# Attention values products with the values stationary in two column tiles, on a hybrid decoder trunk

## The reference

```python
# FoX: 4 heads, own keys and values per head, causal, a forget bias
logits = einsum('bqhd,bkhd->bhqk', qb, k) * scale + Fq[..., None] - Ft[:, :, None, :]
p = softmax(where(causal, logits, -inf)); out = einsum('bhqk,bkhd->bqhd', p, v)
...
# DSA: 4 query heads, one key and one value head, only the 256 best keys of an indexer
p = softmax(logits); out = einsum('bhqk,bqkd->bqhd', p, vg)
...
# sliding window: 4 query heads on 2 key and value heads, the last 128 keys, a sink in the softmax
p = softmax(concatenate([logits, sink]))[..., :-1]; out = einsum('bnhgqs,bnshd->bnqhgd', p, vb)
...
ys = stack([y_a, y_d, y_f, y_s]); proj = einsum('blnc,ncd->blnd', ys, w_branch)
out = sum(sigmoid(g) * proj) @ w_o
```

## Time and profile before

| | |
|---|---|
| median of 3 runs | 1719.34 us (1719.2 to 1725.06) |
| span of the profiled execution | 1720.7 us |
| PE busy | 1674.9 us, 97% of the span |
| DVE, ACT, POOL busy | 62%, 36%, 48% |
| first FoX stretch, from the first to the last turning | 261.2 to 296.0 us |
| second FoX stretch | 340.5 to 374.8 us |
| window units | 376.8 to 406.3 us |
| DSA units | 759.6 to 830.0 us |

### The profile page before, as it was taken

The page is one execution under the profiler, slowest core; times in us unless marked ns, Lnnn a source line. Parts: engine busy times, 40 slices in busy tenths (PEclk is TensorE's granted clock), DMA queues, the critical chain, the costliest instruction groups (busy, mean ns, idle before and its releaser), DMA issues.

```text
span 1720.7 us, 22891 instructions
## 1 busy us (share of the span) xinstructions
PE 1674.9 (97%) x8072; PEld 1394.3 (81%) x8072; DVE 1058.8 (62%) x1756; ACT 612.9 (36%) x1104; POOL 822.9 (48%) x537
## 2 busy tenths in 40 slices
PE   5999999999999999999999999999999999999997
PEld 4877878788888888879888888888888888888886
DVE  7745985565999999567586445743453354345337
ACT  5543326274223222246323454322223222322323
POOL 2421130101436665540387334776567556655855
PEclk9999998999999999999999999999999999999999
DMA  8131141001111111320674412121112012111205
GB/s 345 37 84 39 62 108 28 31 25 45 61 46 46 46 46 50 137 77 1 246 261 159 171 54 94 37 74 49 49 49 73 24 49 73 49 49 49 73 25 208
DMA packets 37600, 138.89 MB, mean 81 GB/s; under 512 B 4640, under 2 KB 4768, under 8 KB 37536
## 3 DMA queue, kind: packets, MB, share of 16 engines
q1 hardware_dynamic: 35296, 130.70, 21.7%
q0 software_dynamic: 2240, 7.34, 1.9%
HBM read 118.10 MB, written 13.63 MB: 77 GB/s over the span
## 4 chain that ended last, share of the span: by engine, by line
PE 87%; DVE 6%; ACT 2%; DMA 1%; SPq 1%; issue 1%; DVEq 1%; POOL 0%; POOLq 0%; ACTq 0%
PE ps L662 25%; PE ps L663 25%; PE ps L664 25%; PE ps L888 4%; PE ps L867 2%; PE ps L789 1%; PE ps L790 1%; DMA region_a<-in_x 1%; PE ps L693 1%; DVE region_c L1966 1%; SPq L549 1%; DVE h_t L1958 0%; DVEq L2016 0%; DVE region_a L2318 0%; DVE top L2012 0%
## 5 line engine op out<-in xcount | busy, mean ns | idle before, releaser
L662 PE MATMUL ps<-h_t,w_t 128*128 128x512 f32 x1112 | 436.8, 393 | 1.8 <-DVE h_t L1958 1.6
L664 PE MATMUL ps<-h_t,w_t 128*128 128x512 f32 x1112 | 433.5, 390 | 0.0
L663 PE MATMUL ps<-h_t,w_t 128*128 128x512 f32 x1112 | 433.5, 390 | 0.0
L662 PEld LDWEIGHTS ps<-h_t,w_t 128*128 128x128 f32 x1112 | 209.2, 188 | 47.3 <-issue 2.5
L1616 POOL TENSOR_TENSOR w_t<-raw,w_t 128x1280 fp32r<-128x1280 f32 (+1 forms) x50 | 141.5, 2830 | 216.1 <-ACT w_t L1197 215.8
L664 PEld LDWEIGHTS ps<-h_t,w_t 128*128 128x128 f32 x1112 | 209.2, 188 | 43.8
L663 PEld LDWEIGHTS ps<-h_t,w_t 128*128 128x128 f32 x1112 | 209.1, 188 | 42.9 <-issue 0.7
L2333 DVE TENSOR_TENSOR y_f<-ps,y_f 128x512 f32<-128x512 f32 x120 | 80.8, 686 | 217.5 <-PE ps L664 217.5
L1775 POOL TENSOR_TENSOR w_t<-raw,w_t 128x512 fp32r<-128x512 f32 x80 | 110.8, 1390 | 135.9 <-ACT w_t L1504 135.6
L2012 DVE MAX8 top<-region_b 128x8 f32<-128x512 f32 (+5 forms) x192 | 159.2, 883 | 20.4 <-issue 19.7
L2015 DVE MATCH_REPLACE8 region_b<-top,region_b 128x512 f32<-128x512 f32 (+5 forms) x192 | 166.4, 877 | 0.0
(11 more groups left out here) (287 smaller groups left out, 3344.8 us busy)
## 6 DMA issues: line engine op xcount, KB each, us to landing
raw<-in_w_ffn SPq DMA_DIRECT2D x46, 512.0 KB, 3.9
raw<-in_w_gates SPq DMA_DIRECT2D x32, 640.0 KB, 4.0
region_b<-in_w_ada SPq DMA_DIRECT2D x33, 512.0 KB, 4.5
region_d<-in_w_ffn SPq DMA_DIRECT2D x20, 512.0 KB, 4.1
raw<-in_w_z SPq DMA_DIRECT2D x18, 512.0 KB, 3.4
region_a<-in_x SPq DMA_DIRECT2D x8, 512.0 KB, 14.8
h_f<-in_w_ada SPq DMA_DIRECT2D x8, 512.0 KB, 8.7
raw<-in_w_o SPq DMA_DIRECT2D x8, 512.0 KB, 3.6
```

What stands on the lines that cost most here:

```text
L662: pe.matmul(o, a_hi, m_hi, start=first, stop=False, skip_group_check=more)
L663: pe.matmul(o, a_hi, m_lo, start=False, stop=False, skip_group_check=more)
L664: return pe.matmul(o, a_lo, m_hi, start=False, stop=last, skip_group_check=more)
```

## The change

The output of a group is now made with channels on partitions from the start: the values are stationary (64 columns), 128 columns of turned probabilities move, and the two heads of a group write the two halves of the partitions of one bank, as two column tiles of the array (`rows_of` 0 and 1). Both units of a pair are multiplied in one go at the pair's end, so a DSA group has two heads now and there are 16 of them. What is turned on PE is no longer the output but the reciprocal of the denominators, spread over 64 columns each (`group_over_den`); DVE then copies the turned reciprocals out of PSUM and multiplies the output with them (`group_norm`, into `y_raw`). For the window that result is final, and its `group_lo` is gone. On PE a round is now: logits of u + 2, `turn_out` and values of u - 1, turning of u. The scratch of the descriptors of POOL's DMAs is halved to 8192 bytes to make room for `y_raw`.

```diff
-            return O_DSA + TT - 1 - b, h == 0, h == HEADS - 1
+            return O_DSA + 2 * (TT - 1 - b) + h // 2, h % 2 == 0, h % 2 == 1
...
+            def turn_out(u):
+                g, _, last = group_of(u)
+                if not last:
+                    return
+                if g >= 2:
+                    pe.wait_ge(s_y_raw, g - 1)
+                pe.wait_ge(s_y_tok, g + 1)
+                for c in range(BT if units[u][0] == "swa" else 1):
+                    mm = pe.transpose(group_bank(u)[:, BW + c * P:BW + (c + 1) * P],
+                                      y_tok[g % 2][:, c * P:(c + 1) * P], ident)
+                mm.then_inc(s_turned, 1)
+
             def values(u):
-                g, first, last = group_of(u)
+                if not group_of(u)[2]:
+                    return
                 pe.wait_ge(s_pt, u + 1)
-                if first and g >= 2:
-                    pe.wait_ge(s_of, g - 1)
...
-                        mm = pe.matmul(bank[:, col * HD:(col + 1) * HD], pt[u % 2][:, c * P:(c + 1) * P],
-                                       vn[:, block_, v0:v0 + HD], start=n == 0, stop=n == len(terms) - 1)
+                    for c in range(b + 1):
+                        for j, rows_ in enumerate(rows_of):
+                            v0 = VF + (h - 1 + j) * HD if kind == "fox" else VD
+                            mm = pe.matmul(bank[rows_, 0:P], vn[:, c, v0:v0 + HD],
+                                           pt[(u - 1 + j) % 2][:, c * P:(c + 1) * P], start=c == 0, stop=c == b)
...
                     if u + 2 < end:
                         logits(u + 2)
-                    turn(u)
+                    if u > u0:
+                        turn_out(u - 1)
+                        values(u - 1)
                     if u >= end - 2:
                         fill(parts_at[2 * (u - end + 2)])
-                    if u - 2 >= u0:
-                        turn_out(u - 2)
-                    if u > u0:
-                        values(u - 1)
+                    turn(u)
...
                     if u >= u0 + 2:
-                        act.wait_ge(s_pv, u - 1)
+                        act.wait_ge(s_pv, group_of(u - 2)[0] + 1)
...
-            def group_norm(u):
+            def group_over_den(u):
...
-                dve.wait_ge(s_pv, u + 1)
+                dve.wait_ge(s_exp, u + 1)
...
-                                  group_bank(u)[:, 0:nh * HD].rearrange("p (h d) -> p h d", h=nh),
-                                  r.unsqueeze(2).broadcast_to((P, nh, HD)), ALU.mult).then_inc(s_y_tok, 1)
+                dve.tensor_copy(y_tok[g % 2][:, 0:nh * HD].rearrange("p (h d) -> p h d", h=nh),
+                                r.unsqueeze(2).broadcast_to((P, nh, HD))).then_inc(s_y_tok, 1)
+
+            def group_norm(u):
...
+                dve.wait_ge(s_pv, g + 1)
+                dst, turned, over_den = group_values(u, y_s)
+                if kind != "swa":
+                    dst = y_raw[:, g % 2, :]
+                order.then_wait(dve.tensor_copy(dst, turned))
+                dve.tensor_tensor(dst, over_den, dst, ALU.mult).then_inc(s_y_raw, 1)
...
                         biased(u + 1)
+                    if u > u0:
+                        group_over_den(u - 1)
                     if u >= u0 + 2:
                         group_norm(u - 2)
...
-    nc = bacc.Bacc("TRN2", target_bir_lowering=False, num_devices=1)
+    nc = bacc.Bacc("TRN2", target_bir_lowering=False, num_devices=1, dynamic_dma_scratch_size=8192)
```

More of the change, by code:

```diff
@@ L83 @@
 O_FOX, O_SWA, O_DSA = 0, 2 * TT, 3 * TT
+O_END = O_DSA + 2 * TT
 MIX0 = 1
@@ L391, in build @@
         s_turned = sem("s_turned")
+        s_y_raw = sem("s_y_raw")
         s_o_hi = sem("s_o_hi")
@@ L594, in _ @@
             for dt, (s, n) in enumerate(((s_logit, after), (s_logit, after), (s_lg, after), (s_t, after - 1), (s_t, after),
-                                         (s_pv, after - 1), (s_pv, after)), 1):
+                                         (s_pv, O_END), (s_pv, O_END)), 1):
                 sp.wait_ge(s, n)
@@ L901, in turn_out, with values @@
                 mm.then_inc(s_turned, 1)
+            def values(u):
+                kind, b, h = units[u]
+                if not group_of(u)[2]:
+                    return
+                pe.wait_ge(s_pt, u + 1)
+                bank = group_bank(u)
+                if kind == "swa":
+                    cs = (0, 1) if b else (1,)
+                    for ch in range(BT):
+                        for n, c in enumerate(cs):
+                            for j, rows_ in enumerate(rows_of):
+                                k0, v0 = (2 * (2 * ch + j) + c) * P, VS + ch * HD
+                                mm = pe.matmul(bank[rows_, ch * P:(ch + 1) * P], vn[:, b - 1 + c, v0:v0 + HD],
+                                               pt[u % 2][:, k0:k0 + P], start=n == 0, stop=n == len(cs) - 1)
+                else:
+                    for c in range(b + 1):
+                        for j, rows_ in enumerate(rows_of):
+                            v0 = VF + (h - 1 + j) * HD if kind == "fox" else VD
+                            mm = pe.matmul(bank[rows_, 0:P], vn[:, c, v0:v0 + HD],
+                                           pt[(u - 1 + j) % 2][:, c * P:(c + 1) * P], start=c == 0, stop=c == b)
+                mm.then_inc(s_pv, 1)
             def attention(u0, n, gate=None, halves=0):
@@ L926, in attention @@
                 fill(parts_at[4])
-                turn_out(end - 2)
+                turn_out(end - 1)
                 values(end - 1)
                 fill(parts_at[5])
-                turn_out(end - 1)
                 fill(4 * KT)
@@ L1315, in group_hi @@
                     return
-                act.wait_ge(s_turned, g + 1)
-                dst, src = group_turned(u, y_hi(1 if units[u][0] == "fox" else 0))
-                act.activation(dst, src, ACT.Copy).then_inc(s_o_hi, 1)
+                act.wait_ge(s_y_raw, g + 1)
+                dst, _, _ = group_values(u, y_hi(1 if units[u][0] == "fox" else 0))
+                act.activation(dst, y_raw[:, g % 2, :], ACT.Copy).then_inc(s_o_hi, 1)
             def exponentials(u):
@@ L2096, in group_norm @@
                     return
-                nh = 2 if kind == "fox" else HEADS
-                dve.wait_ge(s_pv, u + 1)
+                nh = HEADS if kind == "swa" else 2
+                dve.wait_ge(s_exp, u + 1)
                 d, r = den[:, g % 4, 0:nh], rec[:, g % 2, 0:nh]
@@ L2113, in group_lo @@
                     return
[L2114 to L2122 removed]
+                dve.wait_ge(s_pv, g + 1)
[4 more added lines that the diff above has]
+                dve.tensor_tensor(dst, over_den, dst, ALU.mult).then_inc(s_y_raw, 1)
+            def group_lo(u):
+                kind, b, h = units[u]
+                g, _, last = group_of(u)
+                if not last or kind == "swa":
+                    return
+                buf = 1 if kind == "fox" else 0
+                dve.wait_ge(s_o_hi, split_group(u) + 1)
+                dst, _, _ = group_values(u, y_lo(buf))
+                hi, _, _ = group_values(u, y_hi(buf))
+                dve.tensor_tensor(dst, y_raw[:, g % 2, :], hi.bitcast(F32), ALU.subtract).then_inc(s_of, 1)
             def biased(u):
@@ L2168, in attention @@
                         group_lo(u - 3)
+                group_over_den(end - 1)
                 group_norm(end - 2)
```

49 lines of the change are left out of this document (14 added, 35 removed).

## The result

| | before | after |
|---|---|---|
| median of 4 runs each | 1719.72 us (1719.2 to 1725.06) | 1776.67 us (1773.61 to 1783.17) |
| span of the profiled execution | 1720.7 us | 1773.9 us |

The ratio is 1.0328, with a 95% interval of 1.0312 to 1.0344: the change makes the kernel slower by 57 us. I had forecast 1753, and 1738 to 1790.

The account below looks back on a forecast made before the run. PE was taken to bound the kernel, with DVE following; the new wait makes it slower: FoX 5.2, window 7.7, DSA 17.4 and clock 3 sum to 33 us on the 1720.7 span, so 1753 as median, range 1738 to 1790.

Parts of the forecast that it names:

- the wait: Every pair: PE waits 1.5 to 2.5 us for DVE's reciprocals before values and next turning; some 25 us over DSA.
- The products: Values in column tiles: two tiles overlap, 0.216k + 0.21 us for a group of k blocks, 0.432k before.
- PE stays the bound: Rival, attention loops: reciprocals are out before PE finishes the next logits, kernel gains 29 us, 1691; 4 in 100.
- tiles that take turns: Rival, values: column tiles don't overlap, 0.216k more per group, 38 us in all, 1791; 12 in 100.
- both FoX stretches: FoX attention: a pair's loop is 0.676k + 1.57 us for k blocks; 2.6 us longer per stretch, +5.2.
- window: Window units: each unit takes 5.3 us against 4.05 before, over six steps, +7.7 us.
- DSA: DSA attention: DVE's list closes the loop, 0.726k + 2.30 us a pair; 74.9 against 60.5 us, with first and last pairs +17.4.
- clock: DSA pairs of few blocks: half clock on idle PE costs 9 us over k = 4 to 1 if lasting; 3 taken.
- the clock stays low: Rival, DSA units and end of FoX: the whole 9 us and 6 more from larger blocks, 1765; 8 in 100.
- my signs: Observations to confirm the forecast, among them PE's busy share below 93%, DSA turnings alternating, DSA stretch 86 to 91 us.

Follow-up runs that it names:

- run 1: The changed kernel with DVE's reciprocal and spreading copy of unit u-1 moved ahead of bias and addition of unit u+1: 1723.0 us, ratio 1.0008.
- run 2: The changed kernel with PE's order of before, turning of unit u ahead of turned reciprocals and values of unit u-1: 1727.5 us, ratio 1.0038.
- Run 3: The kernel before, own products, with only PE's order changed: turned reciprocals and values ahead of the turning of unit u: 1800.9 us, ratio 1.0458.
- run 4: The changed kernel with a pair's products issued as all blocks of one head, then all of the other: 1802.0 us, ratio 1.0471.
- run 5: The changed kernel with PE's turning ahead of the values and DVE's reciprocal and copy ahead of bias and addition: 1718.7 us, ratio 0.9989.
- run 6: The changed kernel with both moves, on PE's and DVE's order, and a third buffer of turned probabilities: 1712.4 us, ratio 0.9945.
- run 10: The changed kernel with unread products ahead of PE's wait for the reciprocals, 3 per FoX group, 6 per window and DSA group: 1762.7 us, ratio 1.0245.

## Why the prediction was right, and where its sizes were off

**The mechanism was right.** The step that I called the wait is what happens, in the place and the order described: in the changed kernel 24.8 us of it lie over DSA (25 forecast), 53.2 in all. Runs 1 and 2 take it away by two different edits, and with it 54 and 49 of the 57 us. Run 3 puts it into the kernel before without the tiles.

**The products were right.** Values of 8 blocks take 1.90 to 1.97 us a pair (1.94 forecast); the tiles do not take turns (run 4), and that rival falls. The Trainium skill, "TensorEngine Tiling (Array Packing)", Key Properties, says that different tiles load weights and multiply in parallel. The trace agrees where the products alternate between the tiles, and run 4 shows 3.33 us instead of 1.97 where they don't.

**PE stays the bound** did not come, and runs 1, 5 and 6 show that even without the wait the 29 us of that rival are not to be had: with the wait gone the kernel is level with before (and 0.55% below it with a third buffer), since ACT's copy, the buffers and, in DSA, DVE's list take PE's place.

**The sizes.** The medians grew by 57 us and the spans by 53.2, and I had 33. That 1777 lies in the range is in part luck: its upper end was set by tiles that take turns, and they don't. Run 10, with the clock held at 1.00, divides the rest. From the start of the program to the first turning of the second FoX stretch it is 1.4 us longer than before, from there to the first of DSA 15.2 (5.0 to the last turning of FoX, 10.2 behind it), from there to the end 22.7; together 39.3, and 13.8 more without the filling.

| term | forecast | measured |
|---|---|---|
| both FoX stretches | 5.2 | 6.4 (1.4, where before has its low clock, and 5.0) |
| window | 7.7 | 10.2 (7.6 without the 2.6 of the added products in its last two units) |
| DSA | 17.4 | 22.7 |
| clock | 3 | 13.8 (16.4 with these 2.6) |
| sum | 33 | 53 |

*The clock* is the step that failed most. I looked for its fall at the small blocks of DSA and took a third of 9 us; it fell in the window units (0.84) as well, and in DSA already at 6 blocks. The rival "the clock stays low" priced it at 15 us, close to what was measured, but that is luck, since it named other places; I gave it 8 in 100. What I had not asked is what the wait of 1.5 us a pair does to PE's activity: I priced a stall as idle time, and not as a reason for the next products to be slow. That the fall hangs on the wait, runs 1 and 10 show; which measure of PE's activity decides it, none does.

*DSA.* From turning 1 to turning 27 run 10 takes 79.1 us, against 74.9 forecast: 0.32 in each of 13 pairs. The rows above show where. A turning of 8 blocks lasts 1.06 us to the end of its last record, and I had added the hand-over to 0.11 x 8 = 0.88: 0.18 short. From DVE's copy to PE pass 0.14 us (798.79 to 798.93), not 0.05. The turning of the reciprocals holds PE for 0.23 (798.93 to 799.16), not 0.11. The values take 1.90, not 1.94. Together that is 0.35, and the additions, the bias row, the reciprocal and its copy took what I had.

*FoX.* Each pair is 0.37 us longer than forecast, from 7 blocks (6.67 in run 10, 6.30 forecast) down to 2. Over a stretch that makes 5 us where I had 2.6. The sum of both stretches, 6.4 against 5.2, looks better than that only because before's first stretch has a low clock of its own. Which pieces of the longer loop make up the 0.37, I did not work out.

*Window.* The unit was right: 394.79 - 389.43 = 5.36 us in run 10, 5.3 forecast. What was wrong is what it was compared with. I took 4.05 us for each of six units from one interval; in before's trace the six take 3.1, 3.0, 4.3, 4.05, 4.05 and 2.9 us. With their mean of 3.57 the term would have been 6 x 1.73 = 10.4, near the 11.4 by which run 10 is longer over these six steps (32.8 against 21.4). That the whole term, without the added products, still comes to 7.6 is luck: 1.8 us more are lost ahead of the window's first turning, and 5.5 are gained behind the sixth step, where the gate products lie; I had neither.

Of my signs, PE's share was to be below 93% and is 94%. That sign was set wrong: my own numbers, 1674.9 less 29 of 1754 us, give 94%. The intervals of the turnings in DSA alternate by 2.3 and 5.8 us at 8 blocks and 2.1 and 5.7 at 7 (2.2 and 5.6 forecast). DSA takes 100 us instead of 86 to 91, and 93 with the clock held.

## What to carry to other kernels

Halving the cost of a product is worth only what the loop around it leaves: before placing a wait ahead of the next step, look at what stands in front of its releaser on the other engine. Here two small operations behind an addition, and in DSA behind a bias row too, cost 54 us, and moving them ahead on DVE's list gave these back. A stall on PE has a second price, the clock of the work behind it; ask for the busy share of the whole loop, and take the baseline of a term from all its intervals.

## What the runs showed of the hardware

- Column tiles: the two records of a pair start within 0.01 us of each other, and 32 records take 1.97 us: the pairs follow each other every 0.11 us, as fast as one product of 128 float32 columns on the whole array.
- Unused products in a wait made the kernel 14 us faster; nothing reads them, and with them the granted clock was 1.00 in all four windows. The clock fell although no wait of PE at the reciprocals was longer than 3.0 us. The Trainium skill, "TensorE: Matmul & The Clock Gate", HAM oscillation, describes such falls behind long waits of PE for data; here it fell behind waits of 1.5 us on average, one in each group.
